# A hybrid decoder layer in fp32: the 16 learned tokens leave the columns that no output reads

## What is computed

```python
z, xbc, dt_raw, sc_b, sc_c, sc_h, g_ssd, g_sc = split(rmsnorm(x) @ w_in)   # 10,272 columns
xbc = silu(causal_conv4(xbc) + conv_b);  xs, Bm, Cm = split(xbc)
dt = softplus(dt_raw + dt_bias)
y, state = chunked_ssd(xs, dt, -exp(A_log), Bm, Cm)     # a first chunk of 16, then chunks of 128
y = y + xs * D_skip
u = group_rmsnorm(y * silu(z)) * norm_w
y_ssd = u @ w_ssd_out
y_sc = (sc_b * causal_conv3(sc_c * sc_h)) @ w_sc_out
x = x + (sigmoid(g_ssd) * y_ssd + sigmoid(g_sc) * y_sc) @ w_o
x = x + moe(rmsnorm(x))      # 4 groups of 8 experts: best group, then its two best experts
y_prompt = final_rmsnorm(x)[:, 16:]                     # the learned tokens are dropped here
```

## Time and profile before

| | |
|---|---|
| runs | 1313.5 us median of 3 (1313.26 to 1313.94) |
| profiled execution, first to last instruction | 1316.0 us |
| PE busy, PEld busy | 1201.4 us (91%), 1033.6 us (79%) |
| DVE, ACT, POOL busy | 531.9, 386.9, 458.6 us |
| mean granted TensorE clock | 0.969 of full speed |
| moved by DMA | 210.67 MB |

### The profile page before, as it was taken

How to read it: one execution, slowest core, us unless ns; L and a number is a source line. 1 busy time by engine, 2 the same in 40 slices (tenths; PEclk the granted TensorE clock), 3 DMA queues, 4 the chain that set the end, 5 groups by cost and what they waited for, 6 DMA issues and landing times.

```text
span 1316.0 us, 22259 instructions
## 1 busy us (share of the span) xinstructions
PE 1201.4 (91%) x8729; PEld 1033.6 (79%) x8729; DVE 531.9 (40%) x839; ACT 386.9 (29%) x568; POOL 458.6 (35%) x358
## 2 busy tenths in 40 slices
PE   5999999999999999999999999999996979777781
PEld 5999999999986986897698689999995646443340
DVE  5445432002556765685576551014444241121112
ACT  4221114433524433442443352122324001010112
POOL 5444432333543453363345443434320111111200
PEclk8999999998999999999999999999998989999996
DMA  6333322232411620541251132343639999999985
GB/s 157 80 82 80 80 64 65 65 94 62 132 49 59 159 64 16 158 106 33 82 151 50 32 105 81 85 129 107 210 113 347 408 399 397 403 398 396 415 331 161
DMA packets 185566, 210.67 MB, mean 160 GB/s; under 512 B 12166, under 2 KB 161798, under 8 KB 176754
## 3 DMA queue, kind: packets, MB, share of 16 engines
q1 hardware_dynamic: 176626, 193.41, 44.1%
q0 software_dynamic: 5040, 9.72, 3.0%
q10 hardware_dynamic: 3822, 6.39, 1.3%
HBM read 191.56 MB, written 26.57 MB: 166 GB/s over the span
## 4 chain that ended last, share of the span: by engine, by line
PE 73%; DMA 10%; DVE 6%; SPq 5%; issue 3%; ACT 2%; POOL 1%; ACTq 0%; DVEq 0%; POOLq 0%
PE acc L641 47%; SPq L562 5%; PE pTS L1031 4%; PE acc L920 4%; DMA big<-in_w_up 4%; PE acc L1072 2%; DMA ring<-in_w_gate 2%; DMA area<-in_w_up 2%; DVE area L1235 2%; PE pTS L820 2%; PE pY L814 1%; PE pY L838 1%; PE acc L779 1%; PE pO L768 1%; DVE area L1233 1%
## 5 line engine op out<-in xcount | busy, mean ns | idle before, releaser
L641 PE MATMUL acc<-h_parts,ring_parts 128*128 128x328 f32 (+1 forms) x3840 | 548.2, 304 | 6.3 <-DVE area L1280 2.2
L641 PEld LDWEIGHTS acc<-h_parts,ring_parts 128*128 128x128 f32 x3840 | 534.3, 191 | 21.3 <-issue 15.3
L1894 POOL TENSOR_TENSOR ring_parts<-ring,ring_parts 128x1024 fp32r<-128x1024 f32 x112 | 280.5, 2505 | 435.3 <-ACT ring_parts L1602 435.2
L1602 ACT ACTIVATE ring_parts<-ring 128x1024 fp32r<-128x1024 f32 x112 | 118.4, 1058 | 392.5 <-PE acc L641 367.2
L1031 PE MATMUL pTS<-area,big 128*64 128x256 f32 x672 | 105.7, 395 | 18.2 <-DMA area<-in_w_gate 5.4
L641 PE MATMUL acc<-u_parts,ring_parts 128*128 128x264 f32 (+1 forms) x640 | 109.4, 299 | 0.0
L1031 PEld LDWEIGHTS pTS<-area,big 128*64 128x64 f32 x672 | 65.2, 143 | 49.8 <-DMA area<-in_w_gate 8.9
L641 PEld LDWEIGHTS acc<-u_parts,ring_parts 128*128 128x128 f32 x640 | 96.4, 188 | 0.0
L641 PE MATMUL acc<-area_parts,ring_parts 128*128 128x264 f32 (+1 forms) x512 | 91.1, 299 | 0.0
L1235 DVE SCALAR_TENSOR_TENSOR area<-area,xvec 128x616 f32<-128x616 f32 x72 | 84.9, 1179 | 10.5 <-DVE area L1233 0.6
L641 PEld LDWEIGHTS acc<-area_parts,ring_parts 128*128 128x128 f32 x512 | 78.4, 188 | 0.0
(11 more groups left out here) (353 smaller groups left out, 1437.9 us busy)
## 6 DMA issues: line engine op xcount, KB each, us to landing
ring<-in_w_in SPq DMA_DIRECT2D x80, 512.0 KB, 4.0
area<-in_w_gate SPq DMA_DIRECT2D x21, 1024.0 KB, 25.4
area<-in_w_up SPq DMA_DIRECT2D x21, 1024.0 KB
area<-in_w_down SPq DMA_DIRECT2D x21, 1024.0 KB, 23.7
area<-in_state_ssm SPq DMA_DIRECT2D x16, 512.0 KB, 6.9
out<-area SPq DMA_DIRECT2D x16, 512.0 KB, 5.5
ring<-in_w_ssd_out SPq DMA_DIRECT2D x16, 512.0 KB, 4.0
ring<-in_w_gate SPq DMA_DIRECT2D x7, 1024.0 KB, 17.4
```

Of the source, the lines that this page charges most:

```text
L641: m = nc.tensor.matmul(acc[a][:, h, 0:n], w[s][:, k, :], x[:, k, h * HALF:h * HALF + n], start=first and k == 0 and w is w_hi and x is hi, ...
L1602: a_.activation(w_hi[b % 2], w_raw[b % 2], ACT.Copy).then_inc(hi_done, 1)
L1894: gp.tensor_tensor(w_lo[b % 2], w_raw[b % 2], w_hi[b % 2].bitcast(F32), ALU.subtract).then_inc(lo_done, 1)
```

## The change

The 16 learned columns are left out of every step that only reads its own column. The 576 tokens left are taken as two equal halves of 288 (columns 16 to 303 and 304 to 591), which fit a single [2, 288] access; for sc_b they are 256 and 320, since its product goes on to the convolution's layout. From w_o on, the buffers are 576 wide and start at the first prompt token, so the five row tiles are 4 x 128 and 64 (before 80). Blocks with sc_c, sc_h, B, C, x, the dt projection and the chunk loop keep all 592. Beside `pe_block`, the evictions on ACT and DVE, the splits, squares and norms of the same tensors are cut to the columns kept.

```diff
+LIVE = T - N_META
+HL = LIVE // 2
+QT = LIVE // 4
+R_OUT = [P] * 4 + [LIVE - 4 * P]
-DUMP, NO_TOKEN = T, 2048
+DUMP, NO_TOKEN = LIVE, 2048
+EVERY = ((0, HALF), (HALF, T - HALF))
+KEPT = ((N_META, HL), (N_META + HL, HL))
+KEPT_CONV = ((N_META, SEQ // 2), (N_META + SEQ // 2, SEQ // 2 + TS))
+        def acc_kept(a):
+            return a[:, :, 0:HL]
+        def packed(v):
+            return v[:, 0:LIVE].rearrange("p (a b) -> p a b", a=2)
@@ pe_block
-                        n = HALF if h == 0 else T - HALF
-                        m = nc.tensor.matmul(acc[a][:, h, 0:n], w[s][:, k, :], x[:, k, h * HALF:h * HALF + n],
+                        at, n = cut[h]
+                        m = nc.tensor.matmul(acc[a][:, h, 0:n], w[s][:, k, :], x[:, k, at:at + n],
@@ the blocks of the s stage, of o1, of the groups
+                    pe_block(pe, s_block(t, b), b, hT_hi, hT_lo, cut=KEPT_CONV if b % 3 == 2 else EVERY)
+                pe_block(pe, o1_block(f, 0), 0, hT_hi, hT_lo, cut=KEPT)
+                pe_block(pe, o1_block(f, 1), 1, sco_hi, sco_lo, cut=KEPT)
+                    pe_block(pe, g_block(g, b), b, hT_hi, hT_lo, cut=EVERY if b < 6 else KEPT)
+                pe_block(pe, g_block(g, 7), 7, hT_hi, hT_lo, part=0, cut=KEPT)
+                            pe_block(pe, g_block(g, 7 + i), 7 + i, hT_hi, hT_lo, part=0, cut=KEPT)
+                        pe_block(pe, g_block(g, 7 + i), 7 + i, hT_hi, hT_lo, part=1, cut=KEPT)
+                pe_block(pe, g_block(g, 10), 10, hT_hi, hT_lo, cut=EVERY if g + 1 < GROUPS else KEPT)
@@ gate and mix blocks: the same with cut=KEPT; w_o
-                        for h, n in ((0, HALF), (1, T - HALF)):
-                            m = nc.tensor.matmul(acc[a][:, h, 0:n], w[f % 2][:, k, :], x[:, k, h * HALF:h * HALF + n],
+                        for h, (at, n) in enumerate(KEPT):
+                            m = nc.tensor.matmul(acc[a][:, h, 0:n], w[f % 2][:, k, :], x[:, k, at:at + n],
@@ gate_of (ACT); z_gate and the products on DVE likewise
-                a_.activation(g0, a0, ACT.Sigmoid)
-                a_.activation(g1, a1, ACT.Sigmoid).then_inc(acc_free[a], 1)
+                a_.activation(packed(to), acc_kept(acc[a]), ACT.Sigmoid).then_inc(acc_free[a], 1)
@@ split of u (ACT)
-                a_.activation(uT_hi[:, 4 * c:4 * c + 4, :], uT[:, 4 * c:4 * c + 4, :], ACT.Copy).then_inc(u_hi, 1)
+                a_.activation(uT_hi[:, 4 * c:4 * c + 4, N_META:T], uT[:, 4 * c:4 * c + 4, N_META:T], ACT.Copy).then_inc(u_hi, 1)
@@ SP: the residual's rows, 5 loads (before 7), and the output, 5 stores (before 6)
-                if i == 0:
-                    sp.dma_start(yp[0:P - N_META, :], x2[N_META:P, 0, :]).then_inc(y_out, 16)
-                elif i < 4:
-                    sp.dma_start(yp[i * P - N_META:(i + 1) * P - N_META, :], x2[:, i, :]).then_inc(y_out, 16)
+                if i < 4:
+                    sp.dma_start(yp[out_tok(i), :], x2[:, i, :]).then_inc(y_out, 16)
                 else:
-                    sp.dma_start(yp[SEQ - LASTP:SEQ, :], x2[0:LASTP, 4, :]).then_inc(y_out, 16)
-                    sp.dma_start(ys, x2[LASTP:R4, 4, :]).then_inc(y_out, 16)
+                    sp.dma_start(ys, x2[0:TS, 4, :]).then_inc(y_out, 16)
...
```

More of the change, by code:

```diff
@@ L614, in _, with pe_block @@
                 sp.wait_ge(z_y, i + 1)
-                if i == 0:
-                    sp.dma_start(yp[0:P - N_META, :], x2[N_META:P, 0, :]).then_inc(y_out, 16)
-                elif i < 4:
-                    sp.dma_start(yp[i * P - N_META:(i + 1) * P - N_META, :], x2[:, i, :]).then_inc(y_out, 16)
-                else:
-                    sp.dma_start(yp[SEQ - LASTP:SEQ, :], x2[0:LASTP, 4, :]).then_inc(y_out, 16)
-                    sp.dma_start(ys, x2[LASTP:R4, 4, :]).then_inc(y_out, 16)
-            sp.wait_ge(y_out, 16 * 6)
+                if i < 4:
+                    sp.dma_start(yp[out_tok(i), :], x2[:, i, :]).then_inc(y_out, 16)
+                else:
+                    sp.dma_start(ys, x2[0:TS, 4, :]).then_inc(y_out, 16)
+            sp.wait_ge(y_out, 16 * TILES)
             sp.wait_ge(tails_out, 16 * 16)
-        def pe_block(pe, where, b, hi, lo, first=True, last=True, part=None):
+        def pe_block(pe, where, b, hi, lo, first=True, last=True, part=None, cut=EVERY):
             n_, _, a, ause = where
@@ L850, in _ @@
                 pe.wait_ge(s_hs, g * 4 + 3)
-                pe_block(pe, g_block(g, 10), 10, hT_hi, hT_lo)
+                pe_block(pe, g_block(g, 10), 10, hT_hi, hT_lo, cut=EVERY if g + 1 < GROUPS else KEPT)
                 pe.wait_ge(s_hs, g * 4 + 4)
-                pe_block(pe, g_block(g, 11), 11, hT_hi, hT_lo, part=0)
+                pe_block(pe, g_block(g, 11), 11, hT_hi, hT_lo, part=0, cut=EVERY if g + 1 < GROUPS else KEPT)
                 pe.wait_ge(s_so, g + 1)
@@ L858, in _ @@
                     for j in range(4):
-                        m = nc.tensor.matmul(pT[32 * j:32 * j + 32, 0:QT], ones[:, 0:32], sq[:, k, j * QT:(j + 1) * QT],
+                        m = nc.tensor.matmul(pT[32 * j:32 * j + 32, 0:QT], ones[:, 0:32], sq[:, k, N_META + j * QT:N_META + (j + 1) * QT],
                                              start=k == 0, stop=k == GK - 1)
                 m.then_inc(p_gn, 1)
-                pe_block(pe, g_block(g, 11), 11, hT_hi, hT_lo, part=1)
+                pe_block(pe, g_block(g, 11), 11, hT_hi, hT_lo, part=1, cut=EVERY if g + 1 < GROUPS else KEPT)
                 pe.wait_ge(s_rm, g * 2 + 2)
@@ L870, in _ @@
             for n in range(2, 4):
-                pe_block(pe, gate_block(n), n, hT_hi, hT_lo)
+                pe_block(pe, gate_block(n), n, hT_hi, hT_lo, cut=KEPT)
             for f in range(8):
@@ L876, in _ @@
                     pe_block(pe, mix_block(f, h), h, uT_hi[:, 8 * h:8 * h + 8, :], uT_lo[:, 8 * h:8 * h + 8, :],
-                             first=h == 0, last=h == 1)
+                             first=h == 0, last=h == 1, cut=KEPT)
                 if f in (1, 3):
                     for n in range(f + 3, f + 5):
-                        pe_block(pe, gate_block(n), n, hT_hi, hT_lo)
+                        pe_block(pe, gate_block(n), n, hT_hi, hT_lo, cut=KEPT)
             def logits(f):
                 for i in range(TILES):
-                    m = nc.tensor.matmul(pY[0:ROWS[i], i * 36:i * 36 + 36], x2T[:, f, tok(i)], rwl[:, f, :],
+                    m = nc.tensor.matmul(pY[0:R_OUT[i], i * 36:i * 36 + 36], x2T[:, f, out_tok(i)], rwl[:, f, :],
                                          start=f == 0 and i == 0, stop=False)
@@ L889, in row_sums @@
                 for i in range(TILES)[::-1]:
-                    m = nc.tensor.matmul(pY[0:ROWS[i], 180 + i:181 + i], x[:, tok(i)], ones[:, 0:1], start=False, stop=last and i == 0)
+                    m = nc.tensor.matmul(pY[0:R_OUT[i], 180 + i:181 + i], x[:, out_tok(i)], ones[:, 0:1], start=False, stop=last and i == 0)
                 return m
@@ L968, in _ @@
             nc.tensor.matmul(pY[:, 192:192 + NE], ones[:, :], before[:, TILES - 2, :], start=True, stop=False)
-            nc.tensor.matmul(pY[:, 192:192 + NE], ones[0:R4, :], mm[0:R4, TILES - 1, :], start=False, stop=True).then_inc(r_pos, 1)
+            nc.tensor.matmul(pY[:, 192:192 + NE], ones[0:R_OUT[4], :], mm[0:R_OUT[4], TILES - 1, :], start=False, stop=True).then_inc(r_pos, 1)
             def to_rows(u, s):
@@ L1359, in _ @@
                 dve.wait_ge(x_c, f + 1)
-                for h, n in ((0, HALF), (1, T - HALF)):
-                    row = x2T[:, f, h * HALF:h * HALF + n]
-                    x = v.tensor_tensor(row, row, acc[a][:, h, 0:n], ALU.add)
-                x.then_inc(w_x, 1)
+                row = packed(x2T[:, f, :])
+                v.tensor_tensor(row, row, acc_kept(acc[a]), ALU.add).then_inc(w_x, 1)
             scaled(7)
@@ L1685, in z_gate @@
                     split_hi(g_block(g, 6 + k), k)
-                    a0, a1 = acc_parts(acc[a])
-                    d0, d1 = halves(sz[:, k, :])
-                    a_.activation(d0, a0, ACT.Copy)
-                    a_.activation(d1, a1, ACT.Copy).then_inc(acc_free[a], 1)
+                    a_.activation(packed(sz[:, k, :]), acc_kept(acc[a]), ACT.Copy).then_inc(acc_free[a], 1)
                 for c in range(6):
@@ L1778, in _ @@
                 act.wait_ge(x_t, f + 1)
-                a_.activation(x2T[:, f, :], xT_new[:, 0:T], ACT.Copy).then_inc(x_c, 1)
+                a_.activation(x2T[:, f, :], xT_new[:, 0:LIVE], ACT.Copy).then_inc(x_c, 1)
                 if f < 6:
```

143 lines of the change are left out of this document (67 added, 76 removed).

## The result

Each ratio below is of the kernel's timed runs to those of the kernel before on the same chip, with its 95% interval. The changed kernel took 1306.2 us (median of 4 runs, 1304.81 to 1307.44) beside 1313.72 for the kernel before (1313.26 to 1316.43): ratio 0.9938 [0.9924, 0.9952]. It is faster, by 7.5 us, where 13.4 were forecast, and above the range that ended at 1304.5. On a second chip the ratio was 0.9924 [0.991, 0.9938].

A forecast was written before the change was run, and what follows sets the result against it. PE bounds the kernel up to the end of w_o, DMA bytes the expert turns. 8.6 + 2.9 + 0.3 + 0.2 + 1.0 + 0.4 = 13.4 us off 1313.5 gives 1300.1, range 1296.5 to 1304.5.

The forecast's parts named there:

- the term for w_o: w_o stage: last row tile 64 rows not 80 in eight transposes, last addition one instruction; 0.2 us gained.
- the two rates of 0.16 and 0.18: Straight blocks on PE: us saved per block at 0.417 or 0.46 ns a column; 54 blocks give 8.6 or 9.6.
- rival 1: PE matmuls: a column costs only 0.13 ns, a block saves 0.05 us; 5.5 us off, 1308.0; 3%.
- rival 3: Cut blocks: reading from start column 16 or 304 costs more; at 6 ns a matmul 1320.8 us, slower; 2%.
- The groups: Four groups' z blocks: 0.72 us saved each, 2.9 in all; period 113.6 to 112.9.
- the longer first halves: z blocks in groups: first halves grow from 264 to 288 columns, hidden by waits; price at most 2.4 us.
- the forecast's 1.4: Behind w_o: distance from first expert turn to the end shorter by 1.4 us.
- rival 2: Groups' z halves give nothing and 2 us are lost entering the DMA stage through the router; 8.5 off, 1305.0; 12%.
- the z halves: Half blocks of z in the groups: shorter second halves on the chain give 0.72 us a group, 2.9 for four.
- The 1.0 us of the expert stage: Expert turns: gathers and scatters lose 32 of 1184 rows, 0.9, plus 0.1 for rows written and read; between 0 and 1.5.
- the prediction's last sign of being wrong: Expert turns: the forecast is wrong if the first turn is early and the end isn't.
- One more or one less: Stretches of PE clock at 0.50: one more or one less is 1.7 us; no change taken.

The follow-up runs named there:

- before again: The kernel before, unchanged, run and traced a second time: 1315.79 us with a span of 1314.1.
- the early half: Against the kernel before, cuts only up to w_o; w_o and what follows stay at 592 tokens and 80 rows: 1305.11 us, ratio 0.9922.
- the padded one: The changed kernel with its last row tile padded from 64 to 80 rows on PE, all cuts kept: 1299.68 us, ratio 0.9891.
- the late half: The kernel before up to w_o, cut only from w_o on with the 64-row tile: 1319.46 us, ratio 1.003.

## Why the prediction was wrong, point by point

**The step that failed** is the term for w_o under "Part by part, up to w_o": "In w_o: the last row tile is 64 rows and not 80 in eight transposes, and the last addition is one instruction. 0.2." It had the wrong sign: with four changes of shape a turn it costs 0.50 x 8 = 4.0 us against the same kernel at 80 rows (32 changes in all: four in each of seven turns, two in the first, which has no router product yet, and two more in the last for the row sums). I had counted rows, and also only the transposes, while the router's products and sums shrink with the same variable. The trace of before held no 64-row operand in this stage, and the sum allowed the term 0.1 to either side, with no row behind it. With this loss of 4.0 in place of the gain of 0.2 the forecast's 13.4 becomes 9.2, 1304.3 us; the timed gains were 7.5 and, by the second ratio, 10, and 9.2 lies in the interval of both.

The Trainium skill has the rule: "TensorEngine Tiling (Array Packing)", "Key Properties", says that changing the tiling mode, and not only the tile, drains TensorE; under "Available Configurations" it lists 64x128 and 128x64 as modes beside 128x128. The runs here agree, at 64 against 65 rows, and add the price of 0.10 to 0.13 us a change. That it is this drain which takes the time is the page's account; the runs show the price and when it falls due.

**What was right.**
- The columns. With the half clock taken out (1.7 for 3.4 us), the 22 blocks behind the groups went from 144.1 to 140.2, 0.175 us a block: between the two rates of 0.16 and 0.18. Forecast 142.5 for the run with its stretch, measured 141.91. The 12 blocks of o1 took 79.13 where 78.3 were forecast, because the stretch at half clock there was 6.8 us long and not 3.4; five other kernels with halves of 288 had no stretch there, and there the run took 76.55, where 78.3 less 1.7 is 76.6. The first 22 blocks came out at 142.30 for 143.0: the eight cut ones gave 0.25 each, 0.7 us more than forecast, and that isn't explained. The flat column rate (rival 1) is excluded, and so is the price of a start column (rival 3).
- The groups: a period of 112.9, as forecast. The wait ahead of the transposes behind the first half of block 7 went from 0.41 to 0.36 (0.3 forecast) and the one behind group 3 from 1.88 to 2.17 (2.1 forecast), so the longer first halves hid where they should. Both are in the timeline of after, with its last two stores:

```profile
576.41 0.66 PE L771 MATMUL pTS<-ident,area 128*128 128x128 f32 x4 [0.36 <-ACT area L1693]
...
767.75 1.54 PE L665 MATMUL acc<-h_parts,ring_parts 128*128 128x288 f32 x5 [2.17 <-ACT area L1652]
...
1298.79 1.86 SPq L643 DMA_DIRECT2D out<-big  x2
...
1301.70 0.51 SPq L645 DMA_DIRECT2D out<-big  x1
```

- Together: the way to w_o, without half clock, got 12.5 us shorter in the first pair of traces, 0.7 of it ahead of the first block, and 11.3 in the second; the other kernels cut there with halves of 288 agree within 0.6 us of the one after. 10.5 were forecast.
- The forecast's sum, once w_o is mended: 0.9891, 0.9895 and 0.9895 of 1313.5 are 1299.2 and 1299.7 us, where 1300.1 was forecast. That it fits so well is in part luck: the way to w_o gave 1 to 2 us more than the forecast, and behind w_o the traces don't show the forecast's 1.4. In the same way the measured 1306.2 lies near rival 2's 1305.0 without its mechanism: the z halves gave all that was forecast, and the loss sits in w_o.
- Slips in the prediction's numbers that don't change the verdict: the low and high ends of its parts add up to 11.4 and 13.5 ahead of w_o's end, not 11.3 and 13.3. The earlier trace rows shows one stretch at half clock, not two, and the trace has a third, of 6.8 us at 304.8, that it overlooked. And the 3 x 64 KB of rows written and read back would be 0.5 us at 392 GB/s, not 0.1, if all of them fell where DMA is full.

**What can't be told.** The 1.0 us of the expert stage. With 592 rows its turns took 267.1, 266.7 and 266.3 us (before, before again, the early half), with 576 rows between 264.8 and 268.3 in eleven traces, mean 266.4. The bytes are gone, as the queue of gathers and scatters between 1007 and 1271 shows (8.55 MB in the earlier trace rows):

```profile
q0 software_dynamic: 4482, 8.35, 12.5%
```

but the stage varies by 3.5 us at equal work, and its start too: from w_o to the first turn it was 29.1 to 31.5 us in the cut kernels, 29.2 and 29.4 in the two traces of before. Rival 2 said that this entry would give part back. It was 0.9 us longer on the average of the eleven. In the trace after, the first expert turn began 11.3 us earlier and the way from it to the end was 0.3 us longer, not 1.4 shorter: the prediction's last sign of being wrong. Taken together, from the last matmul of w_o to the last expert turn, the eleven took 295.4 to 298.3 us, mean 296.6, where the two traces of before had 296.5 and 295.9: no gain of 1.0 shows. In the trace before, this way ended through a y_sum store of 7.88 us; in the trace after it runs through the router on DVE and the first gather, 5.28 us. That gather took 3.8 to 6.7 us over all cut kernels (3.82 where the way was 29.1 us, 6.70 and 6.63 where it was 31.1 and 31.5), while stores of rows and expert weights kept the DMA engines at 0.91 to 0.93. I didn't test it alone.

**The clock.** Stretches of 3.4 or 6.8 us at level 0.50 came and went near 220, 300 and 767 us, and differ between traces of one kernel (6.8 us and twice 10.2 in the padded one). There were 13.6 us of them in both traces of before and 10.2 in the late half, but 10.2 in both of the changed kernel and 3.4 to 10.2, mean 8.0, in all eleven traces with the way to w_o cut (the early half among them). So there are fewer with the cut, and why isn't shown; between 13.6 and 8.0 us lie 2.8 us of time, a part of the gain that no term of the forecast has. "One more or one less" held for the changed kernel and was too narrow for the others.

## What to carry to other kernels

Cutting rows pays by the column where a busy PE sets the end, but a remainder tile that falls to 64 or less changes the shape of the array: count the changes, not the rows, and try one padded row above 64 where such instructions stand singly between full ones. The cheapest version here streams 576 columns and pads the tile: about 14 us below the kernel before, where the change as written gets 8 to 10. Bound even the small terms from both sides; this one had 0.2, give or take 0.1, and was worth twenty times that the other way.

## What the runs showed of the hardware

- A change between 128-wide operands and one of 64 rows (64x128 weights) or 64 columns (128x64) costs PE 0.10 to 0.13 us, also on the way back, where the profile counts it as busy time of the next matmuls (6.54 for 6.42 us). Two small shapes side by side, 64 rows and then 64 columns, save one change of four.
- 65 rows behave as 80: 7.90 and 7.93 us a turn, with 64 rows 8.43.
- Matmuls of 256 to 328 columns cost 0.45 to 0.46 ns a column in half blocks that stand alone, and no pair of widths that adds up to 576 (256/320, 264/312, 288/288) is cheaper in a steady run than the 1.2 ns by which one and the same kernel differs between two traces (264.4 and 265.6 ns).
- The expert turns, at a DMA share near 1.00, took 264.8 to 268.3 us in eleven traces of equal work there, 264.9 to 266.7 in one and the same kernel, so that a saving of 1 us can't be read from single traces.
